# Head-pair steps in a block-sparse attention stage: paired exponentials, row-tiled score matmuls, and the block gate in the merge's PSUM banks

## What is computed

```
h = rms_norm(x, norm_mix)
q, k, v, u, g_a, g_p = split(h @ w_in)
q, k = rope(rms_norm(q)), rope(rms_norm(k))          # 8 heads of 64
o_attn = moba_attention(q, k, v)   # own block of 256 keys (causal), and the 3 past blocks with the best gate
o_pool = multiscale_pool(u)        # trailing means over 2/4/8/16 tokens, one linear per group
merged = sigmoid(g_a) * (o_attn @ w_up_attn) + sigmoid(g_p) * (o_pool @ w_up_pool)
x = x + merged @ w_out
x = x + square(relu(rms_norm(x) @ w_ff1)) @ w_ff2
# the block gate: gate = q . mean(k over block), past blocks only, the top 3 are kept
```

## Time and profile before

| what | value |
| --- | --- |
| median of 3 runs | 950.29 us (950.02 to 950.58) |
| the profiled execution, its own time | 950.71 us |
| its span on the slowest core (core 7) | 949.6 us |
| spans of the 8 cores | 945.3 to 949.6 us |
| TensorE (PE) matmuls busy | 908.0 us, 96% of the span |
| VectorE (DVE) busy | 461.8 us, 49% |
| ScalarE (ACT) busy | 375.2 us, 40% |
| GpSimd (POOL) busy | 75.4 us, 8% |

### The profile page before, as it was taken

The page is one execution under the profiler, slowest core; times in us unless marked ns, Lnnn a source line. Parts: engine busy times, 40 slices in busy tenths (PEclk is TensorE's granted clock), DMA queues, the critical chain, the costliest instruction groups (busy, mean ns, idle before and its releaser), DMA issues.

```text
span 949.6 us, 17253 instructions; the slowest of 8 cores (945.3 to 949.6 us)
## 1 busy us (share of the span) xinstructions
PE 908.0 (96%) x5772; PEld 466.0 (49%) x5772; DVE 461.8 (49%) x876; ACT 375.2 (40%) x738; POOL 75.4 (8%) x133
## 2 busy tenths in 40 slices
PE   2797999899999999999999999999999999999997
PEld 1354555566677764444444444444444444444443
DVE  2578877555533324344774444444444443444443
ACT  2566666698889872222005344031111221111120
POOL 4212110321000000100001000000000000000000
PEclk9899999999999999999999999999999999999999
DMA  8952034633433435892989804250064100002113
GB/s 187 212 131 68 2 76 89 83 52 69 68 68 57 78 68 117 166 207 73 211 133 158 120 1 62 40 78 1 1 89 64 27 1 1 1 0 80 59 62 156
DMA packets 57895, 76.31 MB, mean 80 GB/s; under 512 B 27792, under 2 KB 46224, under 8 KB 57552
## 3 DMA queue, kind: packets, MB, share of 16 engines
q0 software_dynamic: 24288, 40.28, 28.0%
q1 hardware_dynamic: 33520, 34.92, 13.4%
HBM read 98.41 MB, written 8.39 MB: 112 GB/s over the span
## 4 chain that ended last, share of the span: by engine, by line
PE 87%; DMA 6%; DVE 3%; issue 2%; ACT 1%; SPq 0%; POOL 0%; DVEq 0%; ACTq 0%; POOLq 0%
PE bank L1315 23%; PE bank L1341 23%; PE bank L988 10%; PE bank L429 8%; PE bank L882 6%; PE bank L1225 6%; PE bank L920 3%; PE bank L1002 3%; PE bank L1007 3%; DMA raw<-w_qkvu 3%; DMA raw<-x 2%; DMA raw<-w_slice 1%; PE bank L483 1%; DVE raw L399 0%; DMA raw<-raw 0%
## 5 line engine op out<-in xcount | busy, mean ns | idle before, releaser
L1322 ACT ACTIVATE raw<-bank 128x512 f32<-128x512 f32 x128 | 76.5, 598 | 376.5 <-PE bank L1315 317.9
L1315 PE MATMUL bank<-raw 128*128 128x512 bf16 x1024 | 224.0, 380 | 0.0
L1341 PE MATMUL bank<-raw 128*128 128x512 bf16 x1024 | 223.1, 379 | 0.0
L1315 PEld LDWEIGHTS bank<-raw 128*128 128x128 bf16 x1024 | 100.4, 98 | 121.5 <-issue 2.8
L1341 PEld LDWEIGHTS bank<-raw 128*128 128x128 bf16 x1024 | 100.2, 98 | 120.8
L1324 DVE SCALAR_TENSOR_TENSOR raw<-bank,raw 128x512 bf16<-128x512 f32 x128 | 88.6, 692 | 141.7 <-ACT raw L1322 141.7
L889 ACT ACTIVATE raw<-bank 128x512 bf16<-128x512 f32 (+1 forms) x288 | 146.2, 593 | 22.2 <-PE bank L920 20.3
L1347 DVE SCALAR_TENSOR_TENSOR raw<-bank,raw 128x512 f32<-128x512 f32 x128 | 96.1, 751 | 112.7 <-PE bank L1341 112.3
L429 PE MATMUL bank<-raw 128*128 128x512 bf16 x512 | 124.0, 392 | 12.0 <-DMA raw<-w_qkvu 6.7
L988 PE MATMUL bank<-raw 128*128 128x512 bf16 x512 | 122.5, 379 | 0.7 <-DMA raw<-w_slice 0.7
L882 PE MATMUL bank<-raw 128*128 128x256 bf16 x576 | 98.3, 266 | 2.0 <-ACT raw L889 1.5
(11 more groups left out here) (91 smaller groups left out, 597.1 us busy)
## 6 DMA issues: line engine op xcount, KB each, us to landing
raw<-x SPq DMA_DIRECT2D x32, 512.0 KB, 6.7
raw<-w_ff POOLq DMA_DIRECT2D x16, 1024.0 KB, 12.7
raw<-w_slice POOLq DMA_DIRECT2D x22, 640.0 KB, 7.9
out<-raw SPq DMA_DIRECT2D x16, 512.0 KB, 2.7
raw<-w_qkvu POOLq DMA_DIRECT2D x8, 512.0 KB, 13.7
raw<-raw SPq DMA_DIRECT2D x2, 1024.0 KB, 6.9
raw<-w_out POOLq DMA_DIRECT2D x4, 512.0 KB, 13.2
raw<-c_ind POOLq DMA_DIRECT2D x4, 256.0 KB, 5.8
```

The source lines that it names most:

```text
L1315: t.group("pe", [lambda e, c=c, j=j, bk=bk: e.matmul(bank_f(bk), lhsT=ffw1[s][:, c, j * 128:(j + 1) * 128], rhs=hT[:, c, tg * 512:(tg + 1) ...
L1322: t.op("act", lambda e, bk=bk, si_=si_: e.activation(out=sqz[si_], in_=bank_f(bk), func=AF.Square), reads=hb[bk], writes=[b_sqz[si_]])
L1341: t.group("pe", [lambda e, j=j, bk=bk, hf=hf, i=i: e.matmul(bank_f(bk), lhsT=a1T[ab][:, j, i * 128:(i + 1) * 128], rhs=ffw2[s][:, j, hf * ...
```

## The change

Steps are taken by head pairs: (query block, pair of heads, pair of key tiles), 144 in place of 288, and `LOOK` is 2 pairs in place of 4 steps. A pair's scores lie in two neighbouring banks, 0 and 1 or 2 and 3 by turns, one bank per head. One exponential reads both banks (2 x 512 columns, or 2 x 384 on the diagonal). The probability tiles become 3 of 2 x 512 in place of 5 of 512. In query blocks 0 to 3, and on the diagonal of the others, no bias is needed: there the four score matmuls of a pair contract over the head's own 64 rows (rows 0 to 63 for the even head, 64 to 127 for the odd one), alternating between the halves; elsewhere they take all 128 rows as before. Of the 144 steps, 56 are of the first kind, 32 of them on the diagonal.

With bank 3 gone to the scores, `gate_mm` moves into bank 6 and `gate_tr` into bank 7, the merge's banks: the gate of a token tile is issued right behind the second chunk of a unit's first gate projection (units 0 to 7), the transpose right behind the second chunk of the second one (units 1 to 8). Each stands behind a tanh that reads the same bank. The planner's late tasks share banks 6 and 7 with the projections. 16 units lie in the attention stage in place of 14, one chunk every 1.3 pair steps from step 8 on, and 16 units come after it.

```diff
-        NPT = 5
+        NPT = 3
-        N_ATT = 14
+        N_ATT = 16
-            tpn = "mb" if late else "tp"
+            tpn = "pj" if late else "tp"
-        gate_ps = bank_f(MISC)[:, 128:192].rearrange("p (h n) -> p h n", h=H)
+        gate_ps = bank_f(gbank[0])[:, 0:64].rearrange("p (h n) -> p h n", h=H)
...
-            tps = bank_bf(MISC)[:, 0:128]
+            tps = bank_bf(gbank[1])[:, 0:128]
...
+        steps = [(qb, pr, kp) for qb in range(NB) for pr in range(H // 2) for kp in range(qb + 1)]
-        LOOK = 4
+        LOOK = 2
+        ROW_TILED = True
...
+            b0 = 2 * (si % 2)
+            half = ROW_TILED and (qb < 4 or kp == qb)
             for j in range(2):
                 kt = 2 * kp + j
                 qa = 128 if kp == qb and j == 1 else 0
+                for e_ in range(2):
+                    ksel = kT2 if e_ else kT
+                    r0, r1 = (e_ * 64, e_ * 64 + 64) if half else (0, 128)
+                    fns.append(lambda e, kt=kt, j=j, qa=qa, e_=e_, ksel=ksel, r0=r0, r1=r1: e.matmul(
+                        bank_f(b0 + e_)[:, j * 256:j * 256 + 256 - qa],
+                        lhsT=ksel[r0:r1, pr, kt * 128:(kt + 1) * 128],
+                        rhs=qTz[r0:r1, 2 * pr + e_, q0 + qa:q0 + 256], start=True, stop=True))
...
+            t.op("act", lambda e: e.activation(
+                out=pt[:, :, 0:nc_], in_=psum[:, b0 * 512:b0 * 512 + 1024].rearrange("p (e c) -> p e c", e=2)[:, :, 0:nc_],
+                func=AF.Exp, scale=0.125),
+                reads=hb[b0] + hb[b0 + 1], writes=[b_PT[si % NPT]])
...
             def ga2(u_=u_):
                 g_gate_mm(u_, 0, 6, range(4, 8))
                 g_tanh(6, ga_1, b_ga1)
             chunks.append((0, ga2))
+            if ui < 8:
+                chunks.append(("sel", 8 + ui))
             chunks.append((0, lambda u_=u_: g_gate_mm(u_, 1, 7, range(0, 4))))
...
             chunks.append((0, gp2))
+            if 1 <= ui < 9:
+                chunks.append(("tr", 7 + ui))
...
-        G_START = 14
+        G_START = 8
```

More of the change, by code:

```diff
@@ L253, in build_nc @@
         xslot = [view(D0 + 16 * KB + i * 4 * KB, [128, D], F32) for i in range(NXS)]
-        NPT = 5
-        PT = [view(D0 + 16 * KB + i * KB, [128, 512], BF16) for i in range(NPT)]
-        o_tok = view(D0 + 21 * KB, [128, 2, 512], BF16)
+        NPT = 3
+        PT = [view(D0 + (16 + 2 * i) * KB, [128, 2, 512], BF16) for i in range(NPT)]
+        o_tok = view(D0 + 29 * KB, [128, 2, 512], BF16)
         bias8 = [view(D0 + 28 * KB + i * 256, [128, 128], BF16) for i in range(2)]
@@ L292, in build_nc @@
         wsl = [view(o_, [128, 2560], BF16) for o_ in slot_off]
-        banks = [es.enter_context(nc.psum_tensor("bank%d" % i, [128, 512], F32)) for i in range(8)]
+        psum = es.enter_context(nc.psum_tensor("psum", [128, 4096], F32))
         hb = [[Buf("psbank%d" % i, excl=True)] for i in range(8)]
         def bank_f(i):
-            return banks[i][:, :]
+            return psum[:, i * 512:(i + 1) * 512]
         def bank_bf(i):
-            return banks[i][:, :].bitcast(BF16)
+            return psum[:, i * 512:(i + 1) * 512].bitcast(BF16)
         t = Trk(nc, es)
@@ L696, in build_nc @@
                 bm.opts = [("pe", 0.47, lambda tt=tt, k_=bm, n_=tpn: band_mm(tt, k_.slots[n_]))]
+                if late:
+                    bm.only = gbank
                 tasks.append(bm)
@@ L719, in build_nc @@
                     is_k, tt, m_.slots["qtok"], k_.slots[n_]))]
+                if late:
+                    tr_.only = gbank
                 ev_ = Task("kev" if is_k else "qev", ji + 0.8, [], deps=[tr_], put=[(tr_, tpn)])
@@ L742, in build_nc @@
         km = add("kmean", 45.0, [("dve", 0.6, kmean_fin)], deps=list(k_ev_t.values()))
-        for k_ in tasks:
-            if "mb" in k_.get:
-                k_.deps.append(km)
+        first_pair = km
         add("xdone", 0.0, [("pool", 1.0, x_done)], deps=[hev[tt] for tt in range(NT)])
@@ L888, in emit_qk @@
+            rd = [b_kT[2 * kp], b_kT[2 * kp + 1], b_qT[2 * qb], b_qT[2 * qb + 1], b_kT2h[pr // 2]]
+            if not half:
+                rd += b_ind[pr // 2]
+            t.group("pe", fns, reads=rd, writes=hb[b0] + hb[b0 + 1])
+            nc_ = 384 if kp == qb else 512
             pt = PT[si % NPT]
-            t.op("act", lambda e: e.activation(out=pt[:, 0:nc_], in_=bank_f(sb_)[:, 0:nc_], func=AF.Exp, scale=0.125),
-                 reads=hb[sb_], writes=[b_PT[si % NPT]])
+            t.op("act", lambda e: e.activation(
+                out=pt[:, :, 0:nc_], in_=psum[:, b0 * 512:b0 * 512 + 1024].rearrange("p (e c) -> p e c", e=2)[:, :, 0:nc_],
+                func=AF.Exp, scale=0.125),
+                reads=hb[b0] + hb[b0 + 1], writes=[b_PT[si % NPT]])
@@ L903, in emit_pv @@
         def emit_pv(si):
-            qb, h, kp = steps[si]
-            gi = qb * 3 + h // 3
-            hh = h % 3
-            bk = accb[gi % 2]
+            qb, pr, kp = steps[si]
             pt = PT[si % NPT]
-            fns = []
-            rds = [b_PT[si % NPT], b_v[2 * kp], b_v[2 * kp + 1]]
-            for j in range(2):
-                kt = 2 * kp + j
-                for ql in range(2):
-                    if ql == 0 and kt == 2 * qb + 1:
-                        continue
-                    last = (2 * qb) if ql == 0 else (2 * qb + 1)
-                    o_ = (ql * 3 + hh) * 65
-                    dst = bank_f(bk)[:, o_:o_ + 65]
-                    c0_ = j * 256 + (0 if kt == 2 * qb + 1 else ql * 128)
-                    fns.append(lambda e, dst=dst, c0_=c0_, kt=kt, ql=ql, last=last: e.matmul(
-                        dst, lhsT=pt[:, c0_:c0_ + 128], rhs=v_aug[:, kt, h, :],
-                        start=(kt == 0 and ql == 0), stop=(kt == last), skip_group_check=True))
@@ L941, in o_post @@
                       reads=[b_otok], writes=[b_oT[qb][ql]], transpose=True)
[L944 removed]
         gate_busy = set()
[L946 removed]
         post_at = {}
         for qb in range(NB):
[L949 to L974 removed]
+            post_at.setdefault(first_of[qb + 1] + LOOK - 1, []).append(qb)
         def g_views(k):
@@ L1065, in build_nc @@
             chunks.append((e0, cp))
-        G_START = 14
+        G_START = 8
         chunk_at = {}
         cs_ = float(G_START)
-        G_STEP = (NS + 3.5 - G_START) / len(chunks)
+        n_ch = sum(1 for e0, _ in chunks if not isinstance(e0, str))
+        G_STEP = (NS + LOOK - 0.25 - G_START) / n_ch
         for e0, fn in chunks:
+            if isinstance(e0, str):
+                si_ = chunk_last
+                tt = fn
+                if e0 == "sel":
+                    chunk_at[si_].append(lambda tt=tt: (gate_mm(tt), gate_sel(tt)))
+                    chunk_at.setdefault(si_ + 2, []).append(lambda tt=tt: gate_sel_b(tt))
+                    gate_busy.update(range(si_ - 1, si_ + 4))
+                else:
+                    assert si_ < first_of[tt // 2] - 1, (tt, si_)
+                    chunk_at[si_].append(lambda tt=tt: gate_tr(tt))
+                continue
             cs_ = max(cs_, float(e0))
             si_ = min(int(cs_), NS + LOOK - 1)
+            chunk_last = si_
             chunk_at.setdefault(si_, []).append(fn)
```

138 lines of the change are left out of this document (53 added, 85 removed).

## The result

The changed kernel takes 976.64 us (median of 4 runs, 975.28 to 978.59) against 950.43 us beside it: a ratio of 1.0272, 95% interval 1.0248 to 1.0296. The forecast was 964.7 us in a range of 945 to 979; the sign and the range held, the value was 11.9 us short. The profiled execution took 977.54 us; its slowest core has a span of 976.5 us, 26.9 more than in the earlier trace rows.

The account below looks back on a forecast made before the run. PE was taken as the bound from 201 us on; -2.0 (early stretches) - 5.8 (row pairs) + 6.4 (mode changes) + 15.8 (gate) = +14.4 us on 950.3 gave 964.7 us, range 945 to 979.

Parts of the forecast that it names:

- dear mode changes: Rival: each half/full row change costs 0.16 to 0.37 us, 968.5 to 982 us; 20% together with no side-by-side running.
- halves that do not run side by side: Rival: half-array score matmuls run one after the other, 970.5 us, or 964 with free changes; 20% together with dear changes.
- the likeliest case: The sum as it stands, with mode changes of 0.05 to 0.16 us each: 961 to 969 us, 40%.
- What bounds the kernel: From 201 us on PE is the bound, ScalarE follows (134.9 of 151 us); each us PE idles lengthens the span.
- Gate, +15.8: Gate products and transposes in the merge's banks wait for the tanh: 15 PE stalls of 1.05 us, +15.8 us.
- The rival that these waits are covered: PE had to wait for ScalarE at the gate places anyway, so the gate adds nothing: 942.5 to 948.9 us; 15%.
- Row pairs, -5.8: Score matmuls on array halves side by side save 0.22 us per off-diagonal pair, 0.16 per diagonal one: -5.8 us.
- Mode changes, +6.4: PE switching between half and full rows 64 times from 201 us on, at 0.10 us each: +6.4 us.
- Both rivals on this point: Mode changes free, 958.3 us (20%), or dear, 968.5 to 982 us (20% together with no side-by-side running).
- One exponential per pair, 0 from 201 us on: The joint exponential saves ScalarE 0.08 us a pair, but shortens nothing from 201 us on, since ScalarE waits for PE.
- Two more units, 0: 10.4 us of PE work moves from behind the attention into it; PE bounds both sides, so 0.
- Early stretches, -2.0: Between 163 and 201 us, joint exponentials and row pairs ease ScalarE and PE: -2.0 us, ends 0 and 5.2.

Follow-up runs that it names:

- e_two_exps: The changed kernel with the pair's one exponential split into two, one per head, each waiting for its own bank; 987.53 us, ratio 1.0376.
- a_gate_later: The changed kernel with gate products put behind the merge's next half product and transposes between the other chain's halves, away from the tanh; 960.21 us, ratio 1.0091.
- c_full_rows: The changed kernel with all score products on the full array again, without row pairs or mode changes; 974.88 us, ratio 1.0239.
- b_post_order: The changed kernel with the first two output-channel blocks behind the attention interleaved, so the unit reading the last attention output comes third; 971.53 us, ratio 1.0209.
- g_units14: 14 merge units beside the attention instead of 16, on the changed kernel with gate products and transposes already moved away from the tanh; 953.93 us, ratio 1.0031.
- j_look3: g_units14 with value products three pair steps behind the scores instead of two, and a fourth probability buffer; 953.57 us, ratio 1.0019.
- m_two_otok: j_look3 with full-row scores, plus a second buffer for the normalised output of query blocks 1 and 3; 950.19 us, ratio 0.9984.

## Why the prediction was right or wrong

The sign came from the step that was forecast, the gate. That the time lies in the range is in part luck: the upper part of the range stood there for dear mode changes or halves that do not run side by side, neither of which came, and the likeliest case's own range, 961 to 969, was missed. On the slowest cores the 26.9 us are +0.5 ahead of the attention, +28.8 in it, -2.4 behind it. By the prediction's steps:

- **What bounds the kernel: right.** PE streams where it does not wait, and what it waits is lost: 16.4 us came off when the gate's stalls did. That ScalarE "follows" was too easy: in e_two_exps added work on it reaches PE.
- **Gate, +15.8: right.** 18.1 us by the spacing for 16 places, 17.0 for the 15 that the term counts, 1.13 each for 1.05. The rival that these waits are covered is excluded by a_gate_later.
- **Row pairs, -5.8: right**, -5.5 by the spacing from 204.5 us on, against c_full_rows. The halves do run side by side.
- **Mode changes, +6.4: right.** 0.10 us for each of the two in the timeline, 0.094 in the mean of the 64 places, 6.0 in all. Over the whole attention, against c_full_rows by the spacing: 9.7 us saved by the halves and 10.0 paid for 112 changes, 0.089 each. The rule of the Trainium skill ("TensorEngine Tiling (Array Packing)", Key Properties: a change of mode drains the TensorE) agrees in that a change costs something; the price of the modelled tail, 0.16, which I had put beside it, is too high. Both rivals on this point are out.
- **One exponential per pair, 0 from 201 us on:** not measured apart; the sum below leaves about 1 us for it and for all else. But in the changed kernel's order, with two double banks, its loss costs 10.9 us: the joint exponential pays for the pair steps and does not bring a gain of its own.
- **Two more units, 0: the step that failed.** "PE is the bound on both sides" was true, and I looked for a late slice of weights. What was late is the DMA of the last transposes. In the kernel before, the third unit behind the last value product was the first to read them, at 367.1 us, and PE had 14.7 us of other work until then:

```profile
352.39 3.61 PE L988 MATMUL bank<-raw 128*128 128x512 bf16 x16
...
367.06 1.03 PE L1002 MATMUL bank<-raw 128*128 128x512 bf16 x4
```

After the change it is the second unit, and the cover is 9.6 us. On the slowest core the transposes landed later as well (DMA issues of the changed kernel's slowest core, then of the slowest one before, with the us to landing):

```profile
raw<-raw SPq DMA_TRANSPOSE x2, 12.9
raw<-raw SPq DMA_TRANSPOSE x2, 7.1
```

Cost there: 7.2 us of wait and 2.5 of slow clock, 9.7 in all. The part behind the attention got 2.4 us shorter in place of 10.4, +8.0, since on the slowest core before it was itself 1.8 us longer than on the quickest (592.2 and 590.4). On the median core it got 5.3 shorter, so +5.1. b_post_order and g_units14, which restore the cover in two ways, show it.

- **Early stretches, -2.0: wrong sign.** +2.7 measured, 1.1 of it the first gate wait. I had counted on PE's idle time and ScalarE's saving there, and said of the masks that there are as many. But a pair step chains one exponential and both masks ahead of its value products, and PE waited 3.0 us for the masks (L898). j_look3 took that wait away and met the `o_tok` wait; m_two_otok, with full rows and 14 units, has neither, and the difference to the kernel before is gone.

Terms as measured: early stretches without the first gate 1.6, gate 18.1, row pairs -5.5, mode changes 6.0, units 8.0, ahead of the attention 0.5: together 28.7 for 26.9 us. Of the 1.8 too many, 0.9 is the main stretch of the slowest core before, which was that much longer than on the quickest (151.1 and 150.2 us); 0.9 stays open.

Open: why the transposes landed 4 to 5 us later on one core than on the others (the weight slices under way with them took 12.1 us there, and 8.5 on the slowest core before). The half rows were not tried in the final version.

## What to carry to other kernels

Work that is moved out of a stage where PE is the bound is not free if it was the cover of something that starts at the stage's end; before a move, list which DMA lands in the stretch that the moved work filled. A bank that two users share cost the whole latency of the slower user's queue at each of the 16 places where the second stood right behind the first, and placing the second user half a product later gave nearly all of it back. When several waits stand behind each other, undoing one shows little until the next is undone too.

## What the runs showed of the hardware

- A change between half and full rows of the array cost 0.09 to 0.10 us each way. Two half-row matmuls of 256 columns started together and took the time of one, 0.11 to 0.12 us. A pair with 768 columns saved 0.15 us by the halves, less than the price of two changes (0.18 to 0.19); one with 1024 saved 0.21, a little more.
- In a wait of PE of 7.0 us the granted clock fell to 0.50, 1.2 GHz, and stayed there for 5.3 us of work; this cost 2.5 us on top of the wait. At the same place the other seven cores waited 3.0 to 3.7 us: on five the clock fell as well, for 3.4 to 6.8 us, and on two, with waits of 3.5 and 3.7 us, it did not.
- A stretch of 3.4 us at 0.50 made the attention of one core 1.6 us longer (219.6 for 218.0).
- The same two transposing DMAs landed 7.7 to 9.3 us after issue on seven cores of the changed kernel and 12.9 us on the eighth.
